# Dilated attention in a two-block transformer kernel: two heads at a time, on row groups for the scores and on column groups for the values

## What is computed

```python
def dilated_group(q, k, v, pos, bias_table, window, dilation):
    ...
    s = jnp.einsum('nbqhd,nbkhd->nbhqk', qb, kb,
                   preferred_element_type=jnp.float32) * (DIL_HEAD_DIM ** -0.5) + bias
    s = jnp.where(valid[None, :, None], s, -jnp.inf)
    lse = jax.nn.logsumexp(s, axis=-1)
    p = jnp.exp(s - lse[..., None]).astype(v.dtype)
    o = jnp.einsum('nbhqk,nbkhd->nbqhd', p, vb).reshape(N, Lp, H, Dh)[:, :L]
```

## Time and profile before

| | |
|---|---|
| median of 3 runs | 1681.49 us (1681.36 to 1683.67) |
| the profiled execution | 1683.85 us, its span 1682.0 us |
| busy share of the span | PE 96%, PEld 90%, DVE 66%, ACT 48%, POOL 7% |
| granted TensorE clock, mean | 0.987 of 2.4 GHz |
| dilated stage, first scores to last output step | 1210.12 to 1488.16 us |

### The profile page before, as it was taken

The page is one execution under the profiler, slowest core; times in us unless marked ns, Lnnn a source line. Parts: engine busy times, 40 slices in busy tenths (PEclk is TensorE's granted clock), DMA queues, the critical chain, the costliest instruction groups (busy, mean ns, idle before and its releaser), DMA issues.

```text
span 1682.0 us, 28913 instructions
## 1 busy us (share of the span) xinstructions
PE 1618.8 (96%) x12150; PEld 1518.6 (90%) x12150; DVE 1107.2 (66%) x1396; ACT 811.9 (48%) x1064; POOL 114.6 (7%) x107
## 2 busy tenths in 40 slices
PE   7999999999999999999998999998999999989998
PEld 7999989998999999999887999997999999879997
DVE  5768667775676768777586566657766556455554
ACT  5545444454545454444586444445444544454442
POOL 1040000000140000000020000001110101000000
PEclk9999999999999999999998999999999999999999
DMA  8765466657686547665533276675766544436552
GB/s 283 257 203 191 150 217 225 229 190 247 207 276 208 181 149 242 201 237 192 181 115 101 66 272 228 224 250 196 266 203 214 163 151 151 126 101 200 177 181 93
DMA packets 227169, 325.56 MB, mean 194 GB/s; under 512 B 7672, under 2 KB 195552, under 8 KB 226528
## 3 DMA queue, kind: packets, MB, share of 16 engines
q1 hardware_dynamic: 215624, 313.00, 55.5%
q10 hardware_dynamic: 11416, 10.71, 2.0%
HBM read 314.23 MB, written 9.45 MB: 192 GB/s over the span
## 4 chain that ended last, share of the span: by engine, by line
PE 77%; DVE 8%; ACT 6%; issue 4%; DMA 3%; POOL 1%; SPq 1%; ACTq 0%; DVEq 0%; POOLq 0%
PE bank L521 23%; PE bank L522 23%; PE bank L523 23%; ACT whi L1111 2%; DVE wlo L1569 2%; POOL rstd L1043 1%; PE bank L564 1%; PE bank L598 1%; PE bank L910 1%; PE bank L933 1%; DMA raw<-in_w_ffn_in 1%; PE bank L730 1%; DMA lbias<-forget_sums 1%; PE bank L850 1%; PE bank L660 1%
## 5 line engine op out<-in xcount | busy, mean ns | idle before, releaser
L1569 DVE TENSOR_TENSOR wlo<-raw,whi 128x2048 fp32r<-128x2048 f32 (+1 forms) x241 | 550.3, 2286 | 267.9 <-ACT whi L1111 267.6
L1111 ACT ACTIVATE whi<-raw 128x2048 fp32r<-128x2048 f32 (+1 forms) x241 | 455.7, 1894 | 109.0 <-PE bank L523 80.2
L521 PE MATMUL bank<-hT_hi,whi 128*128 128x256 f32 x1728 | 494.4, 286 | 6.6 <-DVE hT_lo L1682 3.0
L523 PE MATMUL bank<-hT_hi,wlo 128*128 128x256 f32 x1728 | 489.0, 283 | 0.0
L522 PE MATMUL bank<-hT_lo,whi 128*128 128x256 f32 x1728 | 489.0, 283 | 0.0
L521 PEld LDWEIGHTS bank<-hT_hi,whi 128*128 128x128 f32 x1728 | 331.2, 192 | 13.7 <-issue 9.7
L522 PEld LDWEIGHTS bank<-hT_lo,whi 128*128 128x128 f32 x1728 | 331.5, 192 | 1.2
L523 PEld LDWEIGHTS bank<-hT_hi,wlo 128*128 128x128 f32 x1728 | 331.4, 192 | 0.0
L521 PE MATMUL bank<-whi,hT_hi 128*128 128x256 f32 (+1 forms) x944 | 273.9, 290 | 8.9 <-DVE wlo L1569 3.3
L522 PE MATMUL bank<-wlo,hT_hi 128*128 128x256 f32 (+1 forms) x944 | 269.5, 285 | 0.0
L523 PE MATMUL bank<-whi,hT_lo 128*128 128x256 f32 (+1 forms) x944 | 269.3, 285 | 0.0
(11 more groups left out here) (278 smaller groups left out, 1587.4 us busy)
## 6 DMA issues: line engine op xcount, KB each, us to landing
raw<-in_mlp_w SPq DMA_DIRECT2D x64, 1024.0 KB, 5.7
ada_raw<-in_ada_w SPq DMA_DIRECT2D x96, 512.0 KB, 6.5
raw<-in_w_in SPq DMA_DIRECT2D x44, 1024.0 KB, 5.7
raw<-in_w_ffn_in SPq DMA_DIRECT2D x44, 1024.0 KB, 5.2
raw<-in_dil_w_in SPq DMA_DIRECT2D x36, 1024.0 KB, 5.1
raw<-in_w_ffn_out SPq DMA_DIRECT2D x22, 1024.0 KB, 5.0
raw<-in_w_o SPq DMA_DIRECT2D x8, 1024.0 KB, 5.1
bias_near<-near SPq DMA_DIRECT2D x2, 3072.0 KB, 10.3
```

Of the source, the lines that this page charges most:

```text
L521: pe.matmul(dst, lh, rh, start=start, stop=False)
L523: return pe.matmul(dst, ll, rh, start=False, stop=stop)
L1111: act.activation(view(whi[c % SPL], c), view(raw[c % RAW], c), ACT.Copy).then_inc(s_hi, 1)
L1569: dve.tensor_tensor(view(wlo[c % SPL], c), view(raw[c % RAW], c), view(whi[c % SPL], c).bitcast(F32), ALU.subtract).then_inc(s_lo, 1)
```

## The change

- Heads are taken in pairs. `scores` makes the matmuls of both heads in turn: rows 0 to 63 for one, rows 64 to 127 for the other, into two banks.
- The probabilities are divided by their sum ahead of the turn, by DVE, in place in `Ld` (`norm_probs`: two reciprocals, four multiplications of 128x512 per pair). The division of the result is gone.
- `values` holds the values (64 columns) and streams the turned probabilities (128 columns). One head writes PSUM partitions 0 to 63 and the other 64 to 127 of the same bank, so that the result stands turned, and `turn_pair` is gone.
- `Ld` and the bias buffers are four instead of two, `PTd` two instead of one, `Vd` one instead of two. Four heads' bias is loaded ahead of the stage's first split.
- Eight instead of nine projections run ahead of the first scores. From then on each set has nine, in fixed places: between scores and norm, norm and turn, turn and values, and one (first pair) or two (second pair) behind the values. In the last set one projection is left, and the output steps stand in fixed places.

```diff
-            Vd = [sb(f"Vd{i}", [P, NG, TT, 256], at=ph) for i in range(2)]
+            Vd = sb("Vd", [P, NG, TT, 256], at=ph)
...
-            biasb = [sb(f"biasb{i}", [P, TT, BW], at=ph) for i in range(2)]
-            Ld = [sb(f"Ld{i}", [P, TT, BW], at=ph) for i in range(2)]
-            PTd = sb("PTd", [P, TT, BW], at=ph)
+            biasb = [sb(f"biasb{i}", [P, TT, BW], at=ph) for i in range(4)]
+            Ld = [sb(f"Ld{i}", [P, TT, BW], at=ph) for i in range(4)]
+            PTd = [sb(f"PTd{i}", [P, TT, BW], at=ph) for i in range(2)]
...
+            ahead(3 * NG - 1)
+            for j in range(LAST):
+                for p in range(HB // 2):
+                    scores(j, p, left[0])
+                    ahead()
+                    norm_probs(j, p)
+                    ahead()
+                    turn_probs(j, p)
+                    ahead()
+                    values(j, p)
+                    ahead(1 + p)
+            scores(LAST, 0, left[0])
+            ahead()
+            norm_probs(LAST, 0)
+            scores(LAST, 1, None)
+            project_out(0, 1)
+            turn_probs(LAST, 0)
+            project_out(2, 3)
+            norm_probs(LAST, 1)
+            values(LAST, 0)
+            project_out(4, 5)
+            turn_probs(LAST, 1)
+            project_out(6, 7)
+            values(LAST, 1)
+            project_out(*range(8, 20))
...
+                for t in range(TT):
+                    names = [("S", unitd(HB * j + 2 * p + h), t) for h in range(2)]
+                    bks = [begin("a", nm) for nm in names]
+                    for k, (g, kt) in enumerate(blocks(t)):
+                        for h in range(2):
+                            rows = slice(64 * h, 64 * h + 64)
+                            m = pe.matmul(bks[h][:, P * k:P * k + P], qTd[j % 2][rows, g, p, P * t:P * t + P],
+                                          kTd[j % 2][rows, g, p, P * kt:P * kt + P], start=True, stop=True)
...
+                bk = begin("w", ("OT", u // 2), b=own_bank(j, 5 * p))
                 for t in range(TT):
                     for k, (g, kt) in enumerate(blocks(t)):
...
+                        for h in range(2):
+                            m = pe.matmul(bk[64 * h:64 * h + 64, P * t:P * t + P],
+                                          Vd[:, g, kt, HD * (2 * p + h):HD * (2 * p + h) + HD],
+                                          PTd[h][:, t, P * k:P * k + P], start=k == 0, stop=k == 3)
+                end(m, ("OT", u // 2))
...
-            for n in range(2):
+            for n in range(4):
                 bias_load(n)
...
+            def norm_probs(j, p):
+                for h in range(2):
+                    n = HB * j + 2 * p + h
+                    u = unitd(n)
+                    dve.wait_ge(s_exp, 2 * u + 2)
...
+                    dve.reciprocal(rz[:, u % 2, :], zsum[:, u % 2, :]).then_inc(s_rz, 1)
+                    dve.wait_ge(s_rz, u + 1)
+                    for t in range(TT):
+                        dve.tensor_scalar(Ld[u % 4][:, t, :], Ld[u % 4][:, t, :], rz[:, u % 2, t:t + 1], None, ALU.mult)\
+                           .then_inc(s_pn, 1)
```

More of the change, by code:

```diff
@@ L430, in ahead @@
                 for _ in range(n):
[L431 to L459, removed]
+                    project(left.pop(0))
@@ L906, in scores, with turn_probs @@
                     own.extend([(n["w"] + k) % WB for k in range(WB)] + [(n["a"] + 4) % AB + WB])
+            def turn_probs(j, p):
                 for t in range(TT):
[L908 to L916, removed]
-                for t in range(TT):
[L918 to L927, removed]
+                    for h in range(2):
+                        at = HB * j + 2 * p + h
+                        u = unitd(at)
+                        pe.wait_ge(s_pn, 2 * at + t + 1)
+                        bk = begin("a", ("T", u, t), b=own_bank(j, 5 * p + 2 * t + h))
+                        for k in range(4):
+                            m = pe.transpose(bk[:, P * k:P * k + P], Ld[u % 4][:, t, P * k:P * k + P], ident[:, :])
+                        end(m, ("T", u, t))
@@ L964, in project_out @@
                     jobs[nm] = (s_acc, n["acc"]) + jobs[nm][2:]
-            dilated(project, scores, idle, turn_probs, values,
-                    lambda j, p: turn_pair(unitd(HB * j + 2 * p) // 2, own_bank(j, 0)), ready, project_out)
+            def project_out(*at):
+                for step in at:
+                    out_step(step)
+            dilated(project, scores, idle, turn_probs, values, project_out)
             mlp(1)
@@ L2210, in values, with scores @@
-            def values(j, i):
-                finish_head_norm()
[L2212 to L2220, removed]
+            def scores(j, p, _):
+                for h in range(2):
+                    n = HB * j + 2 * p + h
+                    u = unitd(n)
+                    dve.wait_ge(s_bld[n % 4], 32 * (n // 4 + 1))
+                    if n >= 4:
+                        full(dve, ("T", u - 4, TT - 1))
+                    for t in range(TT):
+                        bk = full(dve, ("S", u, t))
+                        dve.tensor_tensor_reduce(Ld[u % 4][:, t, :], bk[:, :], biasb[n % 4][:, t, :], 1.0, NEG, ALU.add, ALU.max,
+                                                 mx[:, u % 2, t:t + 1]).then_inc(drain_sem(("S", u, t)), 1)
+                    for t in range(TT):
+                        emptied(dve, ("S", u, t))
+                    dve.tensor_scalar(nmax[:, u % 2, :], mx[:, u % 2, :], -1.0, None, ALU.mult).then_inc(s_nmax, 1)
@@ L2221, in _, with values, project_out @@
+            def values(j, p):
+                finish_head_norm()
+                at_low(unitd(HB * j + 2 * p) // 2, 2 * j + p, strided)
+            def project_out(*at):
+                for step in at:
+                    if step in (0, 4, 8):
+                        split_ahead(("MO", 1, step // 4))
+            dilated(project, scores, norm_probs, idle, values, project_out)
             add_out()
```

100 lines of the change are left out of this document (48 added, 52 removed).

## The result

The changed kernel takes 1659.27 us (median of 4 runs, 1656.69 to 1663.56). The kernel before took 1682.58 us beside it (4 runs, 1681.36 to 1683.67). The ratio is 0.9864, with a 95% interval of 0.9841 to 0.9887: 23.3 us less, where the prediction said 1663 us. Its profiled execution took 1658.62 us.

The account below looks back on a forecast made before the run. TensorE's queue was taken to bound the sets; 16.8 (sets) - 4.8 (clock) - 1.9 - 1.0 (start) + 9.8 (last set) = 18.9 us less, 1665.0 profiled, forecast as a median of 1663 us, range 1654 to 1673.

Parts of the forecast that it names:

- Scores: TensorE, dilated stage: two heads' scores run side by side on two row groups, 1.98 us a pair instead of 3.96.
- The second rival: Scores: alternating row groups don't run side by side, 1.98 us more for each of eight pairs, 1678 us; chance 0.07.
- Values and the wait behind them: TensorE: a pair's values take 1.98 us side by side, then the projection waits 1.8 us for its bank.
- The first rival: Values: column groups run in turn, 3.97 us a pair, without gaps or their clock cost; 1663 us, sharing the forecast's 0.70.
- the third rival: Values: weight loads stand uncovered, a pair costs 5.7 to 7.5 us, slower than before at 1687 us; chance 0.06.
- The sets: Three sets of the dilated stage: 211.3 us instead of 228.1, 16.8 us less, before the clock's 4.8 us.
- The 1.6 us left to sets 0 and 1 for DVE's ada rows: Sets 0 and 1: a third of their extra waits behind DVE's ada rows was expected to stay, 1.6 us.
- the 4.8: Granted clock in the sets: slow stretches charged at 1.2 us behind four of six new gaps, 4.8 us (0 to 7.2).
- DVE and ACT in the sets: Their work, including the norm, is covered by projections: cost 0, up to 1.5 us per pair if DVE's order slips.
- The start: Stage start: four more DMA issues delay the second chunk's projection by 1.9 us; its gap grows to 4.2 us.
- The 1.0 us for a longer slow stretch: Stage start: 1.0 us added for longer slow clock behind the second chunk's grown gap (0 to 1.7).
- The last set: Last set with the output and one projection: 46.0 us instead of 55.8, 2.0 of it for half clock; 9.8 less.

## Why the prediction was right

The mechanism that carried it was the right one, and the range held the time.

**Scores: right.** 1.98 us for a pair was forecast from the earlier trace rows, where the two row groups follow each other in blocks of four; alternating by matmul they measure 1.99. With one row group it is 3.77. The second rival, rows in turn, is out.

**Values and the wait behind them: right.** Side by side 1.98 was forecast and 1.90 measured, and a wait of 1.8 us against 1.81, six times out of six. The chain read from the earlier trace rows gave the wait: 4.2 us from the end of one projection to the free bank, and 4.31 from the start of the transposes to the next projection now (1225.48 to 1229.79). The first rival, columns in turn, was held to be worth the same time. It is out too, for side by side and in turn differ, 1.90 against 3.64. That it would give the same time came out nearly so (1658.19 us against 1659.27), though in the stage it gives 2.5 us less and not 0.5 more: in turn the values cost 3.78 in place and not 4.0, and the clock that they save is 6.0 and not 4.8. Uncovered weight loads, the third rival and the slower end, are out by the loads' rows, 1.73 us within 1.97 and in turn 3.47 within 3.71. In turn a record costs 3.64 / 32 = 0.114 us, as 1.82 / 16 did before, and not the 0.18 to 0.23 of that rival.

The prediction weighed two statements of the Trainium skill, both in "TensorE: Matmul & The Clock Gate". "Measured speedup vs the span model" gives three column tiles 2.38 times the speed of one; no run here has three, and two gave 3.64 / 1.90 = 1.9 times. "What overlaps and what doesn't" has weight loads overlap running matmuls only where the row group differs. The loads of the two column groups, which share all rows, are covered here (1.73 us within 1.97); the two differ, and the measurement decides.

**The sets: right, by two errors that cancel.** 211.3 + 4.8 = 216.1 us was forecast, 216.39 measured. Without the clock each set takes 70.1 to 70.2 us. That is 210.4 for the three, 0.9 under the 211.3. The 1.6 us left to sets 0 and 1 for DVE's ada rows did not come; these waits are gone whole, and not merely hidden in the new ones, for with the free bank all three sets take 66.45 us and TensorE waits in none. Half clock came four times at 7.31 - 5.82 = 1.49 us each and not 1.2, so 6.0 in all and 1.2 over the 4.8. The count of four is luck: the prediction gave no reason for just four of six, and with one row group it is none.

**DVE and ACT in the sets: right.** No wait for the normed probabilities appears in the sets, and a second norm costs 0.8 us over six pairs.

**The start: right, a little too dear.** A wait of 4.2 us was forecast and 4.34 measured. From the first projection to the first scores it is 57.83 us for eight projections; before, it was 55.66 (1148.61 to 1204.27). That is 2.2 more, where 2.9 was charged. The second chunk's projection stands 10.33 us behind the first instead of 8.24 (its start is 1156.87 and not 1158.8, because this execution came to the stage 2.1 us earlier). The 1.0 us for a longer slow stretch was the mis-sized part. The work behind the wait of 4.34 us is at half clock for 5.8 us instead of 3.4, but the projections behind it wait for head norms anyway.

**The last set: right in kind, mis-sized.** This is the term that put the time 4 us under the forecast. 9.8 us less was forecast, 55.81 - 42.17 = 13.6 measured. Of the 3.8 us, 2.0 are the half clock that was charged and didn't come (the stretch's clock is 1.00), and 1.45 are two waits that were shorter: 0.30 and 1.85 instead of 1.1 and 2.5. DVE and ACT were ahead of the working by about a microsecond; the exponentials, for one, ended 15.9 us behind the start of that set and not 17.0. What the 13.6 us are made of can be told by rows only, since no run puts the old order back. Four heads' scores (7.9 us at 1.98 each) became two pairs' (3.97), their values 3.79 us instead of 7.16, and two turns of the result (0.3) are gone, 7.6 in all. The other 6 are mostly waits and half clock of the old order: its mean clock was 0.90 and is 1.00.

**The sum.** Forecast 18.9, measured in the stage 339.55 - 316.39 = 23.2: 3.8 of the difference are the last set, 0.7 the start, and the sets take 0.3 back. The medians differ by 23.3. So the range held the time although the gain was 4.3 us larger than its sum. Of the parts of the change, runs price the two row groups (6.4 us of the stage) and the two column groups (2.5 us the other way); the rest of the 23.2 is read from rows and has no run of its own.

## What to carry to other kernels

When work on the bounding engine is halved between two uses of the same buffer, count what is left between them against the chain that frees the buffer: here 2.5 us (0.53 of transposes and 1.97 of values) stood against 4.3, and the saving became a wait. Taking that result from another ring of banks gave 17 us back. Matmuls on two row groups, or of two column groups, ran at 1.9 times the speed of the same ones in turn, weight loads included, but they pay only where nothing else ends later. Issuing DMAs cost ACT's queue about half a microsecond each here (eight took 4.1 us), so such a block should not stand ahead of an instruction that the bounding engine waits for.

## What was not expected of the hardware

The same wait is not always followed by the same clock. The wait of 1.81 us behind the values was followed by a slow stretch in four of six places in the changed kernel, in the same four with later biases and with the last set's new order, and in none of six with one row group, where the wait is as long, the projection behind it is the same and only the scores take 1.78 us more. Before the next projection of the start, a wait of 1.86 us was followed by a mean clock of 0.78 in one kernel, and the same one of 1.85 us by full clock in another with the same code up to there. In the last set of the changed kernel 1.85 us was followed by full clock. In the kernel before, 1.51 and 1.39 us were followed by slow stretches, and 1.09 was not the earlier trace rows. So a short wait of TensorE had two prices here, its own length, and that with up to 1.5 us on top, and no row here says beforehand which one it will be. What decides it stays open; no run varied the work right ahead of the wait.
